# Three tile declarations: `small` and `half` cut to the columns that are used

## The reference, cut to what matters

```
first block:   h = rms_norm(x);  proj = h @ w_in
               o_att = attention(q, k, v)              8 heads of 64, relative bias
               o_gdn = gated_deltanet(conv(qkv), z, a, b)
               x = x + rms_norm([o_att, o_gdn] @ w_out)
               x = x + rms_norm(square(relu(rms_norm(x) @ w_up)) @ w_down)
second block:  proj = rmsnorm(x) @ w_in_2
               y_a = (gb * conv(gc * xc)) @ w_a_out;  y_r = (norm(retention(q, k, v)) * silu(g)) @ w_r_out
               x = x + (sigmoid(ga) * y_a + sigmoid(gr) * y_r) @ w_o
               x = x + (silu(h @ w_ff_gate) * (h @ w_ff_up)) @ w_ff_down;  out = rmsnorm(x)
```

## Time and profile before

| | us |
|---|---|
| median of three runs | 979.1 |
| the three runs | 979.42, 975.6, 979.1 |
| the profiled execution | 979.42 |
| its span, first to last instruction | 977.4 |
| TensorE busy | 940.8 (96% of the span) |
| VectorE, ScalarE, GpSimd busy | 567.8, 454.6, 91.7 |
| mean granted TensorE clock | 0.986 of full speed |

### The profile page before, as it was taken

The page is one execution under the profiler, slowest core; times in us unless marked ns, Lnnn a source line. Parts: engine busy times, 40 slices in busy tenths (PEclk is TensorE's granted clock), DMA queues, the critical chain, the costliest instruction groups (busy, mean ns, idle before and its releaser), DMA issues.

```text
span 977.4 us, 13906 instructions
## 1 busy us (share of the span) xinstructions
PE 940.8 (96%) x6068; PEld 848.6 (87%) x6068; DVE 567.8 (58%) x625; ACT 454.6 (47%) x527; POOL 91.7 (9%) x93
## 2 busy tenths in 40 slices
PE   5998989999999999999999999999999999999997
PEld 4998768887999999889998988888888799999996
DVE  4679785376645555667773546455456555354453
ACT  6775345547444443564534233632534544343432
POOL 2005331001000000010030330101100000000000
PEclk9999889999999999999999999999999999999999
DMA  7651521032654445554465434444445444545431
GB/s 273 235 176 53 195 95 26 12 118 94 249 207 183 172 172 192 196 185 165 173 220 188 170 135 178 173 172 171 174 149 191 176 152 172 215 173 207 164 147 43
DMA packets 24220, 159.87 MB, mean 164 GB/s; under 512 B 3240, under 2 KB 3512, under 8 KB 5856
## 3 DMA queue, kind: packets, MB, share of 16 engines
q1 hardware_dynamic: 21888, 152.75, 42.7%
q0 software_dynamic: 2272, 6.24, 1.9%
HBM read 157.91 MB, written 2.63 MB: 164 GB/s over the span
## 4 chain that ended last, share of the span: by engine, by line
PE 85%; DVE 8%; ACT 4%; issue 1%; DMA 1%; POOL 0%; SPq 0%; DVEq 0%; POOLq 0%; ACTq 0%
PE bank L402 39%; PE bank L431 31%; PE bank L456 4%; PE bank L381 2%; PE bank L876 1%; DVE t_wl L1346 1%; PE bank L674 1%; DVE t_cout L1362 1%; PE bank L514 1%; PE bank L697 1%; DVE t_gs L1358 1%; ACT t_wh L944 1%; DMA t_ident<-in_ident 1%; ACT t_hold L952 1%; PE bank L827 1%
## 5 line engine op out<-in xcount | busy, mean ns | idle before, releaser
L1346 DVE TENSOR_TENSOR t_wl<-t_raw,t_wh 128x2048 fp32r<-128x2048 f32 (+1 forms) x144 | 328.4, 2304 | 182.0 <-ACT t_wh L944 181.8
L402 PE MATMUL bank<-t_hh,t_wh 128*128 128x256 f32 x1192 | 340.9, 286 | 0.8 <-DVE t_hl L1362 0.6
L402 PE MATMUL bank<-t_hl,t_wh 128*128 128x256 f32 x1192 | 339.4, 285 | 0.0
L402 PE MATMUL bank<-t_hh,t_wl 128*128 128x256 f32 x1192 | 339.3, 285 | 0.0
L944 ACT CAST t_wh<-t_raw 128x2048 fp32r<-128x2048 f32 (+1 forms) x144 | 269.0, 1899 | 38.1 <-PE bank L402 20.0
L402 PEld LDWEIGHTS bank<-t_hh,t_wh 128*128 128x128 f32 x1192 | 231.0, 194 | 3.9 <-DVE t_hl L1362 2.2
L402 PEld LDWEIGHTS bank<-t_hl,t_wh 128*128 128x128 f32 x1192 | 230.9, 194 | 1.2
L402 PEld LDWEIGHTS bank<-t_hh,t_wl 128*128 128x128 f32 x1192 | 230.9, 194 | 0.0
L431 PE MATMUL bank<-t_wh,t_hh 128*128 128x512 f32 x160 | 64.6, 412 | 0.6 <-DVE t_wl L1346 0.6
L431 PE MATMUL bank<-t_wl,t_hh 128*128 128x512 f32 x160 | 62.1, 396 | 0.0
L431 PE MATMUL bank<-t_wh,t_hl 128*128 128x512 f32 x160 | 62.0, 396 | 0.0
(11 more groups left out here) (292 smaller groups left out, 1230.9 us busy)
## 6 DMA issues: line engine op xcount, KB each, us to landing
t_raw<-in_W SPq DMA_DIRECT2D x143, 1024.0 KB, 4.9
skew<-scr POOLq DMA_DIRECT2D x1, 1536.0 KB, 17.9
t_x<-in_x SPq DMA_DIRECT2D x2, 512.0 KB, 4.1
t_T<-skew POOLq DMA_DIRECT2D x8, 128.0 KB, 2.4
out<-t_xt SPq DMA_DIRECT2D x4, 256.0 KB, 2.1
t_tab<-in_tab POOLq DMA_DIRECT2D x1, 640.0 KB, 7.6
t_raw<-in_W SPq DMA_DIRECT2D x1, 512.0 KB, 7.7
t_T<-skew POOLq DMA_DIRECT2D x8, 64.0 KB, 2.2
```

What stands on the lines that cost most here:

```text
L402: m = e.matmul(bank[b][:, c * S:c * S + S], W[w][:, h, k * 128 * nt + c * 128:k * 128 * nt + c * 128 + 128], H[a][:, k, :], start=first, s ...
L1346: e.tensor_tensor(M.wl[:, h, 0:n], M.raw[:, r, 0:n], M.wh[:, h, 0:n].bitcast(F32), ALU.subtract).then_inc(q.sem, q.tick(("lo", i)))
```

## The change

`small` is declared with 208 columns in place of 256, and `half` with 2 in place of 128. The slices that picked these columns at the setting of `half` and at the load of `small` become whole tiles.

```diff
-    M.small = sb(top, "small", [128, 256])
+    M.small = sb(top, "small", [128, NSM])
     st = M.st = sb(top, "st", [128, 128])
-    M.half = sb(top, "half", [128, 128])
+    M.half = sb(top, "half", [128, 2])
...
-            e.memset(M.half[:, 0:2], -0.5).then_inc(q.sem, q.tick("half"))
+            e.memset(M.half[:], -0.5).then_inc(q.sem, q.tick("half"))
...
-            e.dma_start(M.small[:, 0:NSM], A["small"]).then_inc(LD["small"], 16)
+            e.dma_start(M.small[:], A["small"]).then_inc(LD["small"], 16)
```

## The result

| | before | after |
|---|---|---|
| median us (9 runs each) | 979.1 | 984.23 |
| lowest and highest | 975.57, 981.38 | 981.11, 984.55 |
| ratio to before, 95% interval | | 1.0065 (1.0052 to 1.0078) |
| the profiled execution, span | 979.42, 977.4 | 984.16, 982.2 |
| TensorE busy us | 940.8 | 942.7 |

The change made the kernel slower by 0.65%, some 6.4 us; the forecast was 979.1 us, with 981.6 as the upper end. The medians of the nine runs differ by 5.1 us. The ratio rests on more runs (33 of the kernel after are on record), and the text goes by it; its interval, 5.1 to 7.6 us, holds both numbers.

What follows compares the result with a forecast made beforehand. TensorE's pace was taken to bound the kernel (busy 940.8 of 977.4 us, 85% of the chain). All terms were 0: the profiled 979.42 us plus 0.0 is 979.4, less 0.3 to the median gives 979.1, range 974.8 to 981.6.

Steps and rivals of the forecast that it cites:

- The steps on `half`, the roots and the load of `small`: GpSimd's setting of `half`, the 18 roots reading it, the load ahead of `ident`: same work as before, 0 us each.
- The waits on transfers: Four waits, for `ident`, `raw`, `x` and `scr`; none of these transfers writes a moved tile; a new such wait would refute.
- the step on the addresses: Tiles from `hold` on start 672 bytes lower, switching between 0 and 32 modulo 64; taken as 0, ends -2.0 and +2.0 us.
- What a start at 32 modulo 64 costs can be read in this trace: Tiles at 0 and 32 on TensorE, VectorE and ScalarE compared; at most 9 ns, or 1.3%, apart on VectorE.
- The pairs of lines 674, 695 and 697: Plain float32 matmul operands at 0 and 32 modulo 64: equal load and stream times, pace difference below 0.3 ns a matmul.
- at most 0.3 ns each: Bound on the change in each of 1,032 weight loads of split activations at lines 431 and 456; 0.3 us either way.
- The term that was entered as 0.3 us: The bound for all 1,032 moved weight loads at lines 431 and 456 together, either way; taken as 0.
- They have cover besides ... so a load may grow by 40 ns before the pace changes: At line 431 a slot is 228 ns and a load 188 ns, so 40 ns of growth would stay hidden.
- TensorE's weight loads get dearer: Lines 431 and 456, 1,032 slots: loads at 32 modulo 64 outgrow the slot; 989.4 us at 238 ns a load; chance 0.03.
- The smallest loss that it said could be told: At lines 431 and 456, 4.7 ns a slot, a load of 233 ns: 0.5%, or 4.9 us, against no change.
- The step on vector and scalar work: Vector and scalar steps on the chain, 117 us together: moved tiles change them by 1.3% at most; taken as 0.
- The 1.5 us bound: The most that the vector and scalar steps on the chain could gain or lose if all changed by 1.3%.

Runs made afterwards that it cites:

- g4_low32: The kernel before the change, with only the low halves `ml`, `yl`, `rlo` 32 bytes further; one execution, 986.75 us.
- f1_h32: The kernel before the change, with `hh` and `hl` 32 bytes further and every other tile keeping its start modulo 512; 971.18 us, ratio 0.9916.

## Why the prediction was wrong, step by step

The prediction had 979.1 us, from 974.8 to 981.6, and the kernel took 984.23. The steps on `half`, the roots and the load of `small` held: the memset took 99 ns, the roots 554 at the median against 556, `ident` landed after 7.74 us for 7.75. The waits on transfers were the four of the earlier trace rows again, so none on a transfer into a moved tile. What failed was the step on the addresses, at "What a start at 32 modulo 64 costs can be read in this trace".

- I took the wrong variable. I compared tiles by their own start modulo 64. The runs showed that the distance between the two operands of one matmul counts, and that 4 bytes of it are enough. By that measure the trace of before held no comparison at all for the split tiles: `hh` and all ten tiles of the phases stood at distance 0 from `wh`, and so did every row of lines 431, 456 and 402.
- I carried a result from one kind of operation to another. The pairs of lines 674, 695 and 697 are plain float32 matmuls of 128 columns. They did show no difference, and after the change they showed none again (3.77 us). The prediction said itself that no row showed a split operand at 32, and then put "at most 0.3 ns each" into the sum. The term that was entered as 0.3 us was 6.5.
- "They have cover besides ... so a load may grow by 40 ns before the pace changes" was a wrong picture. The load's record stayed at 188 ns and the slot grew by 6. So the slot isn't the longer of the two records, and a bound on the load's record bounds nothing. Where in the slot the time goes, the records don't show.

The rival "TensorE's weight loads get dearer" named the place (lines 431 and 456, 1,032 slots) and the count rightly, and its shape of evidence, line 431 longer and line 402 not, is what came. The smallest loss that it said could be told, 4.7 ns a slot, is near the 6.3 that came. Its mechanism, a longer load past its cover, is not what the records show (188 ns, where it wanted 233), and at 0.03 it was far too cheap for a case in which no row of the trace existed.

The step on vector and scalar work held: on the two executions the 36 instructions of line 1362 that write `cout` took 479 and 476 ns at the median, and those that write `sqb` 691 and 691 on average. The 1.5 us bound was not needed.

The Trainium skill, in "TensorE: Matmul & The Clock Gate", section "Step-by-step: what each phase is for", says that TensorE reads its two operands over independent ports, and that loading the next weights takes no read bandwidth from the matmul that runs. By that one would expect no distance between the operands to matter. The runs here disagree with that expectation, by up to 6.7 ns a matmul in the table above. They don't show what is read by which port, nor that the ports are shared: that the load of the next weights and the running stream get in each other's way is a reading that fits, argued and not shown. The 231.2 to 232.5 ns of g4_low32 fitted none of the three simple forms of it.

## What to carry to other kernels

A declaration that is cut, padded or moved is an edit of every tile behind it. Where TensorE sets the pace and its two operands come out of separate tiles, write down their distance modulo 256 before and after, and where it changes, time it. Here the distances were worth +6.5 us of 979 in the change, and -8 us with 32 bytes of padding ahead of `hh` (f1_h32). The best distance differed between the two shapes and was measured for these operands alone. And where no row of the trace has the changed combination, the bound is not the spread of the rows that happen to be there.

## What was not expected of the hardware

With these float32 operands of the split type, a 512-column matmul with its 128x128 load takes 227.5 ns at a distance of 0 modulo 256 between activations and weights and up to 234.2 elsewhere. A 256-column one, with the weights stationary, takes 119.9 ns at 0, 116.7 with the activations 32 bytes further and 117.8 with 64. Plain float32 matmuls of 128 columns took 3.77 us for 32 before and after the change. The loads' records showed none of it (188 ns at the median before and after).
